# Scale vector of the first layer: from 64 matmuls over its weights to vector passes and eight ones products, with its loads on the scalar engine's queue

## The reference

```python
c_act = jax.nn.silu(c)
for l in range(DEPTH):
    mod = c_act @ w_ada[l] + b_ada[l]
    sh1, sc1, g1, sh2, sc2, g2 = [m[:, None, :] for m in jnp.split(mod, 6, axis=-1)]
    h = rms_norm(x, norm1_g[l]) * (1.0 + sc1) + sh1
    proj = h @ w_in[l]
    ...
```

## Time and profile before

| | |
|---|---|
| time, median of 3 runs | 1947.29 us (1946.86 to 1948.07) |
| profiled execution | 1950.46 us |
| its span in the trace | 1948.8 us |
| mean granted clock of TensorE | 0.924 |
| TensorE busy, matmuls | 1725.1 us (89%) |
| VectorE busy | 1005.3 us (52%) |
| ScalarE busy | 863.5 us (44%) |
| GpSimd busy | 1165.8 us (60%) |
| share of TensorE in the chain that ended last | 71% |
| transfers | 302.71 MB, 155 GB/s in the mean |

### The profile page before, as it was taken

How to read it: one execution, slowest core, us unless ns; L and a number is a source line. 1 busy time by engine, 2 the same in 40 slices (tenths; PEclk the granted TensorE clock), 3 DMA queues, 4 the chain that set the end, 5 groups by cost and what they waited for, 6 DMA issues and landing times.

```text
span 1948.8 us, 33455 instructions
## 1 busy us (share of the span) xinstructions
PE 1725.1 (89%) x13290; PEld 1660.3 (85%) x13290; DVE 1005.3 (52%) x1772; ACT 863.5 (44%) x1411; POOL 1165.8 (60%) x476
## 2 busy tenths in 40 slices
PE   8978998979888999778999888888999895769999
PEld 8978988869888999778988778887999894669999
DVE  3457666456325886557666536424882247334400
ACT  2244444544335663244444454334664442324532
POOL 1346954545365889456865454455888683036886
PEclk8788999989899999888999998899999998578999
DMA  7334743436343558444754355444665652024664
GB/s 261 101 115 152 251 139 130 141 130 225 109 143 126 184 196 286 132 120 135 246 175 137 119 163 163 153 129 119 183 185 179 209 174 87 1 80 137 184 184 131
DMA packets 85513, 302.71 MB, mean 155 GB/s; under 512 B 9840, under 2 KB 12528, under 8 KB 85104
## 3 DMA queue, kind: packets, MB, share of 16 engines
q1 hardware_dynamic: 85360, 300.59, 48.3%
HBM read 299.50 MB, written 1.05 MB: 154 GB/s over the span
## 4 chain that ended last, share of the span: by engine, by line
PE 71%; DVE 15%; ACT 4%; issue 4%; DVEq 3%; DMA 1%; POOL 1%; SPq 0%; ACTq 0%; POOLq 0%
PE gemm_bank L1426 58%; PE turn_bank L1533 2%; DVE ada_acc L735 2%; ACT w_hi L404 2%; PE turn_bank L1503 1%; DVE conv L735 1%; PE outp_bank L1521 1%; PE score_bank L1426 1%; PE score_bank L1503 1%; DMA ada_w<-in_w_ada 1%; POOL w_lo L386 1%; DVE rstd_row L755 1%; DVE idx_score L735 1%; DVE probs L922 1%; PE outp_bank L1568 1%
## 5 line engine op out<-in xcount | busy, mean ns | idle before, releaser
L386 POOL TENSOR_TENSOR w_lo<-w_raw,w_hi 128x1024 fp32r<-128x1024 f32 x472 | 1165.6, 2476 | 771.4 <-ACT w_hi L404 770.9
L404 ACT ACTIVATE w_hi<-w_raw 128x1024 fp32r<-128x1024 f32 x472 | 492.3, 1046 | 767.2 <-PE gemm_bank L1426 738.0
L1426 PE MATMUL gemm_bank<-h_hi,w_hi 128*128 128x256 f32 x2112 | 617.8, 293 | 79.2 <-DVE h_lo L735 28.9
L1426 PE MATMUL gemm_bank<-h_lo,w_hi 128*128 128x256 f32 x2112 | 609.2, 288 | 0.0
L1426 PE MATMUL gemm_bank<-h_hi,w_lo 128*128 128x256 f32 x2112 | 608.6, 288 | 0.0
L1426 PEld LDWEIGHTS gemm_bank<-h_hi,w_hi 128*128 128x128 f32 x2112 | 417.8, 198 | 88.2 <-DVE h_lo L735 30.1
L1426 PEld LDWEIGHTS gemm_bank<-h_lo,w_hi 128*128 128x128 f32 x2112 | 417.8, 198 | 0.1
L1426 PEld LDWEIGHTS gemm_bank<-h_hi,w_lo 128*128 128x128 f32 x2112 | 417.2, 198 | 0.0
L1426 PE MATMUL gemm_bank<-w_hi,h_hi 128*128 128x256 f32 (+2 forms) x704 | 207.2, 294 | 18.4 <-DVE h_lo L735 8.0
L735 DVE SCALAR_TENSOR_TENSOR conv<-gemm_bank,params_sb,conv 128x255 f32<-128x255 f32 (+1 forms) x320 | 139.5, 477 | 140.7 <-ACT conv L567 69.8
L1426 PE MATMUL gemm_bank<-w_lo,h_hi 128*128 128x256 f32 (+2 forms) x704 | 202.7, 288 | 0.0
(11 more groups left out here) (276 smaller groups left out, 2407.4 us busy)
## 6 DMA issues: line engine op xcount, KB each, us to landing
w_raw<-in_stream SPq DMA_DIRECT2D x458, 512.0 KB, 3.6
ada_w<-in_w_ada SPq DMA_DIRECT2D x80, 512.0 KB, 4.7
ada_first<-in_w_ada SPq DMA_DIRECT2D x16, 512.0 KB, 10.5
w_raw<-in_stream SPq DMA_DIRECT2D x8, 256.0 KB, 2.7
alibi_sb<-in_alibi SPq DMA_DIRECT2D x1, 1920.0 KB, 7.2
rows_sb<-in_rows SPq DMA_DIRECT2D x1, 1536.0 KB, 10.5
residual<-in_x_t SPq DMA_DIRECT2D x1, 1024.0 KB, 7.4
out_x<-residual SPq DMA_DIRECT2D x4, 256.0 KB, 4.4
```

The lines of the kernel that those rows point to most:

```text
L386: nc.gpsimd.tensor_tensor(w_lo[:, s, 0:n], w_raw[:, s, 0:n], w_hi[:, s, 0:n].bitcast(f32), ALU.subtract).then_inc(lo_ready, 1)
L404: A(w_hi[:, s, 0:n], w_raw[:, s, 0:n], ACT.Copy).then_inc(hi_ready, 1)
L1426: ins = M(o, a, b, start=first and i == 0, stop=last and i == len(passes) - 1, skip_group_check=True)
```

## The change

The scale of the first layer is now made as the other ten vectors are: VectorE multiplies and adds eight tiles of rows, and TensorE sums over the partitions with eight ones products. The host lays the scale's weights out by rows of inputs; the shift keeps its blocks. In `ada_first` the shift's tiles are 0 to 7 now, and the scale's 8 to 15. The scale's tiles are issued by ScalarE, ahead of its tanh; SyncE issues x right behind c, then tiles 0 and 1, tiles 2 to 7 behind the small inputs, and chunk 0 behind those. On TensorE the eight shift columns come first, with the sum of squares behind the fourth, and the ones products last. VectorE spreads its eight passes over the set-up work: two before the wait for the constants, two behind each half of the sine's arguments, two behind `sin_arg`. They use row 1 of `ada_acc`.

```diff
@@ SyncE
             sp.dma_start(c_act[:], c_col).then_inc(c_full, 16)
+            sp.dma_start(XT[:], x_t.rearrange("(k p) t -> p k t", p=P)).then_inc(x_full, 16)
             for i in range(2):
-                load_first(i)
-            sp.dma_start(XT[:], x_t.rearrange("(k p) t -> p k t", p=P)).then_inc(x_full, 16)
-            for i in range(2, 4):
                 load_first(i)
...
-            for i in range(4, ADA_FIRST - 2):
+            for i in range(2, KT):
                 load_first(i)
             load_chunk(0)
-            for i in range(ADA_FIRST - 2, ADA_FIRST):
-                load_first(i)
@@ ScalarE
+            for i in range(KT, ADA_FIRST):
+                nc.scalar.dma_start(ada_first[:, i, :], w_ada0[i]).then_inc(first_full[i // 2], 16)
             act.wait_ge(c_full, 16)
             A(small[:, 0:KT], c_act[:], ACT.Tanh, scale=0.5).then_inc(c_ready, 1)
@@ VectorE, norm
-                        dve.wait_ge(first_used, ADA_FIRST)
+                        dve.wait_ge(first_used, KT)
                         mods(0, KT, shift_ps)
@@ VectorE, start
             V.tensor_scalar(c_act[:], small[:, 0:KT], 0.5, None, ALU.mult).then_inc(c_silu, 1)
+            def scale_rows(tiles):
+
+                for k in tiles:
+                    acc = ada_acc[:, 1, :]
+                    if k % 2 == 0:
+                        dve.wait_ge(first_full[(KT + k) // 2], 32)
+                    dve.drain()
+                    if k == 0:
+                        V.tensor_scalar(acc, ada_first[:, KT, :], c_act[:, 0:1], None, ALU.mult).then_inc(scale_rows_done, 1)
+                    else:
+                        stt(acc, ada_first[:, KT + k, :], c_act[:, k:k + 1], acc, ALU.mult, ALU.add).then_inc(scale_rows_done, 1)
+
+            scale_rows(range(2))
             dve.wait_ge(in_full, 80)
...
                 V.tensor_scalar(r, r, -3.1415925, None, ALU.max)
+                scale_rows(range(2 + 2 * i, 4 + 2 * i))
             dve.drain().then_inc(sin_arg, 1)
-            dve.wait_ge(first_used, KT)
+            scale_rows(range(6, KT))
+            dve.wait_ge(scale_summed, 1)
             mods(KT, KT, mod_ps[:, KT:2 * KT])
@@ TensorE
-            def ada_first_column(a):
-
-                i = a - KT if a >= KT else a + KT
+            def shift_column(i):
+
                 if i % 2 == 0:
                     pe.wait_ge(first_full[i // 2], 32)
                 for k in range(KT):
-                    out = mod_ps[:, a:a + 1] if a >= KT else shift_ps[:, a:a + 1]
-                    ins = M(out, ada_first[:, i, k * P:(k + 1) * P], c_act[:, k:k + 1], start=k == 0, stop=k == KT - 1)
+                    ins = M(shift_ps[:, i:i + 1], ada_first[:, i, k * P:(k + 1) * P], c_act[:, k:k + 1], start=k == 0, stop=k == KT - 1)
                 ins.then_inc(first_used, 1)
+
+            def scale_sum():
+
+                pe.wait_ge(scale_rows_done, KT)
+                for j in range(KT):
+                    ins = M(mod_ps[:, KT + j:KT + j + 1], ada_acc[:, 1, j * P:(j + 1) * P], ones[:, 0:1], start=True, stop=True)
+                ins.then_inc(scale_summed, 1)
...
             pe.wait_ge(c_silu, 1)
-            for a in range(KT, 2 * KT):
-                ada_first_column(a)
-                if a == KT + 5:
+            for i in range(KT):
+                shift_column(i)
+                if i == 3:
                     square_sum_x(0, 0)
-            for a in range(KT):
-                ada_first_column(a)
+            scale_sum()
             pe.wait_ge(set_up, 1)
@@ host
-    first = wa[0, :, 0:2 * D].reshape(KT, P, 2, KT, P).transpose(2, 3, 1, 0, 4)[::-1].reshape(ADA_FIRST, P, D)
+    first = np.concatenate([wa[0, :, 0:D].reshape(KT, P, KT, P).transpose(2, 1, 0, 3).reshape(KT, P, D),
+                            wa[0, :, D:2 * D].reshape(KT, P, D)])
```

More of the change, by code:

```diff
@@ L249, in build @@
         first_full = [sem(f"first_full{i}") for i in range(ADA_FIRST // 2)]
-        first_used = sem("first_used")
+        first_used, scale_rows_done, scale_summed = sem("first_used"), sem("scale_rows_done"), sem("scale_summed")
         in_full, prm_full, tab_full, out_full = sem("in_full"), sem("prm_full"), sem("tab_full"), sem("out_full")
```

## The result

The median of 20 runs is 1951.35 us after the change and 1946.96 us before it, measured on the same chip. The ratio is 1.0025 with a 95% interval of 1.0015 to 1.0035, so the change costs 4.9 us (2.9 to 6.8). A second comparison of the same two kernels gave 1.0029 (1.0016 to 1.0043). How far to trust a per mille: the kernel before, compared with itself in the same way, came out at 0.9988 (0.9976 to 1.0000).

A forecast was written before the change was run, and what follows sets the result against it. TensorE's chain up to the first projection was taken as the bound; columns, squares and ones products, delayed by loads, reach 51.1 us, plus 16.65 of bare chain gives 67.8 against 67.73, hence 1947.3 us; range 1941.5 to 1951.5.

The forecast's parts named there:

- The step that failed: Whole kernel: all later layers hang only on the first projection's start, 67.73 us before the change.
- the difference that was to carry over: Whole kernel: less than 0.1 us on the projection's start passes unchanged to the median, giving 1947.3 us.
- my signs of being wrong altogether: In the changed profile: first column before 9.5 us, or a span difference that isn't that of the projection's start.
- the clock pattern that I had counted on: TensorE's sum of squares and next 32 records: 10.51 us as measured before, with the short stretch at the high level.
- Equal bytes: Start's loads: both queues move the same bytes, tiles 0 and 1 at 14.9 us; chance 0.38.
- The second rival: Start's loads: pieces pass one for one, x is starved, tiles 0 and 1 at 20.0 us, time 1950.8; chance 0.15.
- the stall that I had forecast: TensorE between second and third column: a wait of 1.5 us for tiles 2 and 3, landing at 23.35 us.
- first rival: Start's loads: sync queue served first, with two thirds of the bytes 1943.0 us, at the bound 1940.4; chance 0.24.
- The third rival: ScalarE held in its eight issues: at 2.98 us each c_act comes at 26.6 us, time 1957; chance 0.10.
- the bare chain with its tail: Between ones products and projection: 14.07 us of uncovered VectorE chain plus 2.58 us to the projection, 16.65 together.
- allowed 1.5 us: TensorE behind the sum of squares: high clock stretch missed or longer, 1.5 us either way in every case.
- The 10 us that I said the sums would bring without the queue: Start with nothing late in loading: projection at 57.8 us, a gain of 10 us.

The follow-up runs named there:

- e8: The changed kernel once more, unaltered, for a second profile; ratio to the kernel before 1.0029.
- e7: The changed kernel with x laid out by partition so it travels in few long pieces, order unchanged; ratio to the kernel before 1.0004.
- e2: The changed kernel with x issued behind tiles 0 and 1, both queues kept; ratio to the kernel before 1.0011.
- e1: The changed kernel with all loads back on the sync queue in the order of before, sums kept; ratio to the kernel before 0.9965.
- e3: The changed kernel with the scalar queue's eight issues held until tiles 2 and 3 have landed; ratio to the kernel before 0.9978.
- e4: The changed kernel with ScalarE's w_hi loop put ahead of the norm's square root; ratio to the kernel before 0.9974.
- p2: The changed kernel with 24 extra VectorE drains at its start, in the wait for c_act; ratio to the kernel before 0.9993.
- p3: The changed kernel with one queue in the order of before, w_hi loop first and 24 extra VectorE drains; 1933.61 us, ratio to the kernel before 0.9923.
- p1: The kernel before with 16 extra VectorE drains in its wait for c_act, none of the change; ratio to the kernel before 0.9998.

## Why the prediction was right and wrong

The median came out 1951.35 us where 1947.3 was forecast, and the ratio of 1.0025 (1.0015 to 1.0035) is a loss where I had forecast none. The time lies just inside the range and a little above the line of 3.9 us up to which I had called it no change, a case to which I gave 0.60; to a slower kernel I had given 0.18.

**The step that failed** is "Everything later hangs on that moment (...) and nothing in it is timed by anything else. So the sum has one question", and with it the difference that was to carry over. The projection's start was forecast at 67.8 us and lies at 66.5 to 69.8, mean 68.4, which is 0.8 us later than in the kernel before. Another 3.3 us come from the attention of the second block, where GpSimd waits 103.4 to 103.5 us in place of 100.1; the two make 4.1 of the 4.9 us measured. No rival named this stage, and I had put everything behind the start at nothing without a row that showed it. One of my signs of being wrong altogether did, a difference of the span that isn't that of the start. But the span fell by 1.4 us and the start by 1.2 in the first profile, which looked like agreement, and only repeated runs showed that it wasn't. That the forecast of the start came within 0.6 us of the mean is in part luck: with the clock pattern that I had counted on, e8, it was 1.7 us too early, and the pattern of the first profile brought it 1.3 us below the forecast.

**The loads.** Equal bytes was the wrong split, the mis-sized term of the start. Tiles 0 and 1 were forecast at 14.9 us and the first column at 15.05; it started at 18.76 and 18.53. The second rival, pieces one for one, has the mechanism, as e7 and the counts show; it forecast 20.0, as it took all of the scalar queue's pieces to pass ahead of tiles 0 and 1, and the columns started 1.2 us sooner, since x had got the lead of some 360 pieces that e8 shows. Of the 3.7 us by which the first column was late, 1.5 were offset by the stall that I had forecast and that didn't come: tile 3 landed at 23.79 us (forecast 23.35), before the first two columns were done, and the third column started at about 25.6 (forecast 23.45). That x's small pieces hold it back was right; that the sync queue gets two thirds of the bytes or all (first rival) was wrong. The rate was right: 357 GB/s up to 9.5 us, then 401, 398 and 407, against 382 and 410 in the earlier trace rows. A second queue brought no bandwidth here.

**The issues.** The eight issues of the scalar engine were done at 5.27 us and c_act was there at 7.25 (forecast 4.3 to 8.6, and 6 to 11). The third rival, held issues, didn't occur on this engine; it did on SyncE, with one issue of 3.86 us and 7.96 us for the six tiles behind it. By e2 and e7 that cost TensorE nothing. The changed kernel's timeline:

```profile
0.74 4.53 ACTq L527 DMA_DIRECT2D ada_first<-in_w_ada  x8
...
5.89 3.86 SPq L338 DMA_DIRECT2D params_sb<-in_params  x1
...
9.80 7.96 SPq L327 DMA_DIRECT2D ada_first<-in_w_ada  x6
```

**TensorE and VectorE.** The ones products took 3.43 us in the chain (forecast 3.41), 64 records 13.79 (13.66), the bare chain with its tail 66.51 - 50.12 = 16.39 (16.65). VectorE's multiply-and-add passes took 1.28 us each, or 2.67 a pair (1.3 each), and ended at 35.4 us (31.7), since the last of the small inputs landed at 21.4 us where 18.1 was forecast: no cost, as forecast, for TensorE asked at 46.5. Squares with the columns behind them took 14.1 us (5.03 + 9.10) in the first profile and 17.3 in e8, forecast 10.51 + 6.83 = 17.34: here the clock decides, and the first profile lies 3.2 us below the forecast where I had allowed 1.5 us. The granted clock in the earlier trace rows is no guide to this: it reads 1.00 at 9.5 to 24 us, where a record takes 0.215 us, and 1.00 again at 34 to 36 us, where one takes 0.10. The pace of the records is what tells the level there. The 10 us that I said the sums would bring without the queue are there: e1 starts the projection at 57.55, forecast 57.8.

**What is shown and what isn't.** Shown: the start is set by how the queues share (e1, e2, e3, e7), and the collision with GpSimd costs some 7 us on the bare path (e4). Shown too: 16 more VectorE instructions that do nothing bring the gap and the long wait into the kernel before (two profiles of two), and 24 more in kernels with the change's sums take the gap and most of the wait out (three of three). Not shown is how the count does it. The gap and the short high level go together in 17 of the 19 profiles, but not in p2 and p3, which have no gap and 10.2 us; so the gap of 0.26 us doesn't account for it. What makes the gap, why p1's start is 3 us early, and which pattern of the clock a start gets, stay open.

## What to carry to other kernels

Before loads go to a second queue, ask what they will pass: the engines were full, the queues took turns by single pieces, and the queue with the smallest pieces lost, with the tiles behind them that were wanted first; leave bulk that is needed late behind the early tiles on one queue, or hold it until they have landed. When a chain loses its cover, look for what stretches it and move that away; here moving one loop brought the projection 7.4 us forward, where the change itself had moved it by about 1 us. And when a total moves by 0.2%, compare stages over several profiles of both kernels, also far from the edit, and test with instructions that do nothing before the difference is put down to the edit's work.

## What the runs showed of the hardware that was not expected

- Two queues with work took turns by single pieces of 1, 4 or more KB: 357 to 331, 233 to 241 and 201 to 204 pieces in 4 us each, and 397 of 401 runs a single piece long in the last of these. In one us near the start (4 to 5 us, e8) it was 369 to 10.
- Sixteen drains near the start of VectorE's program lengthened a stretch 1.6 ms later by 3.4 us (waits of 103.54 and 103.51 against 100.1), with a gap of 0.26 us and a high level of TensorE's clock of 10.2 us in place of 17.1. Twenty-four more in the changed kernel took most of it back (101.00 and 100.31), once with a high level of 10.2 us and a sooner next rise, once with 17.1.
- The pattern of TensorE's clock was the same in that stretch in all five profiles of before (17.1 us high) and in all nine of the changed kinds without drains (10.2), while in the start it varied between profiles of the same kernel (3.4 or 6.8 us at the high level, 3 us of time).
